# A blocked linear recurrence on one Trainium2 core: rewritten on 64x64 quarters of TensorE, with the tiles of 128 tokens in one pipeline

## The reference, cut to the recurrence

```
def _rwkv7_scan(r, w, k, v, a, b):           # [1, T, 8 heads, 64], state S is 64x64 per head
    def step(S, inp):
        r_t, w_t, k_t, v_t, a_t, b_t = inp
        sa = einsum('bhij,bhj->bhi', S, a_t)
        S = S * w_t[:, :, None, :] + sa[..., None] * b_t[:, :, None, :] + v_t[..., None] * k_t[:, :, None, :]
        y = einsum('bhij,bhj->bhi', S, r_t)
        return S, y
```

## Time and profile before

| | us |
|---|---|
| median of 3 runs (lowest, highest) | 3048.98 (3047.99, 3054.2) |
| the profiled execution, own time | 3055.45 |
| its span in the trace | 3053.7 |
| first instruction of the recurrence stage | 2567.17 |
| its last copy, L1819 | 2866.86 |

### The profile page before, as it was taken

How to read it: one execution, slowest core, us unless ns; L and a number is a source line. 1 busy time by engine, 2 the same in 40 slices (tenths; PEclk the granted TensorE clock), 3 DMA queues, 4 the chain that set the end, 5 groups by cost and what they waited for, 6 DMA issues and landing times. The chain is left out here.

```text
span 3053.7 us, 45425 instructions
## 1 busy us (share of the span) xinstructions
PE 2787.8 (91%) x18805; PEld 2297.6 (75%) x18805; DVE 1259.1 (41%) x2065; ACT 774.0 (25%) x1468; POOL 305.3 (10%) x256
## 2 busy tenths in 40 slices
PE   9799999999977898979999999996989987999866
PEld 8699999999965655758888888875767853888555
DVE  5333333333342567352333333336233334454546
ACT  6311111211151178242111111112111122222221
POOL 1100000000030034020000000005000001222102
PEclk9899999999998999979999999997999987999978
DMA  3211111111036400331111111113102100000032
GB/s 133 83 42 42 61 42 41 41 56 48 21 120 147 165 2 14 107 115 55 42 41 61 42 41 62 42 56 133 39 21 90 49 12 6 3 3 3 3 117 96
DMA packets 57934, 175.51 MB, mean 57 GB/s; under 512 B 7742, under 2 KB 15455, under 8 KB 56624
## 3 DMA queue, kind: packets, MB, share of 16 engines
q1 hardware_dynamic: 57778, 173.27, 17.3%
HBM read 146.30 MB, written 26.36 MB: 57 GB/s over the span
## 5 line engine op out<-in xcount | busy, mean ns | idle before, releaser
L769 PE MATMUL f0gu<-b1XH,f0w0H 128*128 128x346 f32 (+1 forms) x528 | 170.2, 322 | 13.5 <-DVE f0w0L L697 13.5
L712 DVE TENSOR_TENSOR f1hf<-f1sg,f1gu 128x512 f32<-128x512 f32 x44 | 30.3, 688 | 341.3 <-ACT f1sg L665 341.3
L723 DVE TENSOR_TENSOR Y<-f0dn,Y 128x512 f32<-128x512 f32 (+1 forms) x180 | 124.0, 689 | 113.6 <-PE f0dn L793 112.6
L771 PE MATMUL f0gu<-b1XH,f0w0L 128*128 128x346 f32 (+1 forms) x528 | 170.2, 322 | 0.0
L771 PE MATMUL f0gu<-b1XH,f0w1L 128*128 128x346 f32 (+1 forms) x528 | 169.7, 321 | 0.0
L770 PE MATMUL f0gu<-b1XL,f0w0H 128*128 128x346 f32 (+1 forms) x528 | 169.7, 321 | 0.0
L712 DVE TENSOR_TENSOR f0hf<-f0sg,f0gu 128x346 f32<-128x346 f32 (+1 forms) x66 | 34.1, 517 | 328.8 <-ACT f0sg L665 328.8
L769 PE MATMUL f0gu<-b1XH,f0w1H 128*128 128x346 f32 (+1 forms) x528 | 169.4, 321 | 0.0
L770 PE MATMUL f0gu<-b1XL,f0w1H 128*128 128x346 f32 (+1 forms) x528 | 169.0, 320 | 0.0
L769 PE MATMUL f1gu<-b1XH,f1w0H 128*128 128x512 f32 x352 | 139.2, 396 | 11.7 <-DVE f1w0L L697 11.7
L723 DVE TENSOR_TENSOR Y<-f1dn,Y 128x512 f32<-128x512 f32 x160 | 109.2, 690 | 90.7 <-PE f1dn L793 90.7
(11 more groups left out here) (391 smaller groups left out, 6521.2 us busy)
## 6 DMA issues: line engine op xcount, KB each, us to landing
f0raw<-in_w_gate_up SPq DMA_DIRECT2D x44, 512.0 KB, 5.3
f1raw<-in_w_gate_up SPq DMA_DIRECT2D x44, 512.0 KB, 5.2
residual<-Y SPq DMA_DIRECT2D x32, 512.0 KB, 2.8
Y<-in_w_ada SPq DMA_DIRECT2D x8, 1536.0 KB, 6.3
f0rawd<-in_w_down SPq DMA_DIRECT2D x22, 512.0 KB, 3.6
f1rawd<-in_w_down SPq DMA_DIRECT2D x22, 512.0 KB, 3.6
w_in_b_raw<-in_w_in_b SPq DMA_DIRECT2D x17, 512.0 KB, 3.6
w_in_a_raw<-in_w_in SPq DMA_DIRECT2D x12, 512.0 KB, 4.2
```

What stands on the lines that cost most here:

```text
L712: dve.tensor_tensor(hf[:, i, 0:w], sg[:, i, 0:w], gu[:, i, 1, 0:w], ALU.mult).then_inc(s["mul"], 1)
L723: dve.tensor_tensor(y, dn[0:r, (par * ND + i) % 4], y, ALU.add).then_inc(s["acc"], 1)
L769: pe.matmul(o, wH[c][:, j, k], xh, start=(k == 0), stop=False)
L771: last = pe.matmul(o, wL[c][:, j, k], xh, start=False, stop=(k == KC - 1))
```

## The change

The stage keeps its mathematics, and its operations are laid out anew:

- Member 1 of each pair is stored with its chunks exchanged (`at(e, q)` is `rows(q)` for e = 0 and `rows(1 - q)` for e = 1). So `p`, one of the two products of `xx`, `ab`, `ak`, `tx`, `wt` and the Gram matrices `rbk` go to all four quarters; the other product of `xx` and `mv`, `uu`, `sa`, `st`, `y` still use two at a time. A third Gram product per pair and chunk gives the triangular matrix already turned, so GpSimd's masking step moves to VectorE (`xm`).
- The transposes become ordinary float32 products with 64x64 identities, 64 per tile where there were 16 transposes of 128x128. `cum` is 8 products of 64 rows instead of 4 of 128. The state S is stored as 64-column blocks, and its products are 64x64. `rb`, `rk` and `y` are computed for each chunk alone.
- The ten groups (five levels by two pairs of heads `g`) become ten "halves". A pass over the ten halves holds the inverse of tile t, the chain and close of tile t-1, and the decays and start of tile t+1. On TensorE a half is: the other tiles' work, then `product(t, h)`, then `update(t, h - 1)`. On VectorE `added(h - 2)` stands first in half h, so an addition stands one half behind its update.
- VectorE and ScalarE operate on both members at once where they did each member by itself; GpSimd's `Uo` covers 128x512 elements instead of twice 128x256.
- The masks are loaded by two DMAs that write 64-column pieces at intervals of 128 columns.

```
+        def at(e, q):
+            return rows(q if e == 0 else 1 - q)
...
+                src = ins["cst"][:, C_TRIX64:C_END].rearrange("p (l t) -> p l t", t=H)
+                for i in range(2):
+                    sp.dma_start(cst[:, :, i], src).then_inc(s_in, 16)
...
+                def start(t):                                   # GpSimd
+                    da.wait(pool, t, "xm")
+                    pi.mark(pool.tensor_tensor(turned(t), turned(t), wide(eye), ALU.add), "eye")
+                    other(t, 1)
...
+                def added(t, h):                                # VectorE
+                    px.wait(dve, t, f"x{h}")
...
+                        if h < 2:
+                            if t:
+                                added(t - 1, HL + h - 2)
+                        elif t < NT:
+                            added(t, h - 2)
+                        if h == 0 and more: decayed(t + 1, "at")
+                        if h == 1 and more: decayed(t + 1, "bt")
+                        if h == 2 and more: decayed(t + 1, "kt")
+                        if h == 3: applied(t - 1, 0); masked(t + 1)
+                        if h == 4 and t: stepped(t - 1, 0); reads(t - 1)
+                        if h == 5: applied(t - 1, 1); decayed(t + 1, "rt")
+                        if h == 6 and more: keys(t + 1)
+                        if h == 7 and t: stepped(t - 1, 1)
...
+                def product(t, h):                              # TensorE
+                    po.wait(pe, t, f"u{l}")
+                    if h >= 2:
+                        dl.wait(pe, t, f"a{h - 2}")
+                    for cc in range(2):
+                        for q in range(2):
+                            for e in range(2):
+                                mm = pe.matmul(inv[at(e, q), g, e, ...], Uo[rows(q), slot(t, l), g, e, o], Xi(t, e, c, q), start=True, stop=True)
...
+                def update(t, h):
+                    al.wait(pe, t, f"m{h}")
+                    for cc in range(2):
+                        if l < LV - 1:
+                            for q in range(2):
+                                for e in range(2):
+                                    pe.matmul(inv[rows(q), g, e, ...], XT(t, e, c, q), mid[at(e, q), g, e, o], start=True, stop=True)
+                        for q, e in ((0, 0), (1, 0), (1, 1), (0, 1)):
+                            mm = pe.matmul(inv[at(e, q), g, 0, ...], mid[at(e, q), g, e, o], XT(t, e, c, q), start=True, stop=True)
...
+                steps = {1: ("ys0",), 3: ("sa0",), 4: ("st0", "rbk"), 5: ("sa1", "ys1"), 6: ("y0",), 7: ("st1",), 8: ("y1",)}
+                for t in range(NT + 1):
+                    for h in halves:
+                        if h == 0 and more: cum(t + 1)
+                        if h == 2 and t: closed(t - 1)          # wt, uu
+                        if t:
+                            for n in steps.get(h, ()): chain(t - 1, n)
+                        if h == 3: inner(t + 1)                 # ab and its turned copy
+                        if h == 6: keys(t + 1)                  # ak
+                        if h == 7: inverse_start(t + 1)         # tx
+                        if h == 8: turn(t + 1, (kk, ab), "tab")
+                        if h == 9: turn(t + 1, (k, v), "tkv")
+                        if h == 5 and t < NT: values(t)         # mv
+                        if t < NT: product(t, h)
+                        if h: update(t, h - 1)
+                        elif t: update(t - 1, HL - 1)
```

More of the change, by code:

```diff
@@ L1754, in recurrence_stage @@
[L1754 to L1760, removed]
@@ L1761, in recurrence_stage @@
-        dc = marks("dve_chain", ["sa0", "rb0", "rb1", "sx00", "sx01", "s00", "s01", "rk0", "rk1", "sa1", "sx10", "sx11", "s10", "s11"])
+        halves = range(HL)
+        pa = marks("pe_pre", ["cum", "ab", "ak", "tx", "tab", "tkv"])
+        pp = marks("pe_p", [f"p{h}" for h in halves])
+        px = marks("pe_x", [f"x{h}" for h in halves])
+        pm = marks("pe_mv", ["mv"])
+        pw = marks("pe_w", ["wt", "uu"])
+        pd = marks("pe_chain", ["ys0", "sa0", "st0", "rbk", "sa1", "ys1", "y0", "st1", "y1"])
@@ new lines, in recurrence_stage @@
+        aa = marks("act_pre", ["eex", "eneg", "ein", "xi", "tab", "tkv"])
+        al = marks("act_mid", [f"m{h}" for h in halves])
+        am = marks("act_mv", ["mv"])
+        aw = marks("act_w", ["wt", "uu"])
+        ad = marks("act_y", ["y"])
+        da = marks("dve_pre", ["at", "bt", "kt", "lt", "xm", "rt", "ak"])
+        dl = marks("dve_add", [f"a{h}" for h in halves])
+        dd = marks("dve_chain", ["sa00", "sa01", "sx0", "s0", "rb", "rk", "sa10", "sa11", "sx1", "s1"])
+        po = marks("pool_u", [f"u{l}" for l in range(1, LV)])
@@ L1796, in _ @@
                 pool.wait_ge(s_in, 32)
-                pool.tensor_scalar(tris[:, :], tri[:, :], -0.6065306597126334, None, ALU.mult).then_inc(s_c, 1)
-                for t in range(NT):
[L1800 to L1812, removed]
+                pool.tensor_scalar(tris[:, 0], cst[:, 2 + LV, 0], -0.6065306597126334, None, ALU.mult).then_inc(s_c, 1)
@@ L1814, in _ @@
+                def start(t):
+                    da.wait(pool, t, "xm")
+                    pi.mark(pool.tensor_tensor(turned(t), turned(t), wide(eye), ALU.add), "eye")
+                    other(t, 1)
+                start(0)
+                for t in range(NT):
+                    for l in range(2, LV):
+                        other(t, l)
+                    if t + 1 < NT:
+                        start(t + 1)
             @block.scalar
             def _(act):
[L1816 to L1819, removed]
@@ L1830, in _ @@
[L1830 to L1835, removed]
-                        else:
[L1837 to L1858, removed]
@@ new lines, in stepped @@
+                def stepped(t, q):
+                    pd.wait(dve, t, f"st{q}")
+                    pd.wait(dve, t, "ys1" if q else "ys0")
+                    dd.mark(dve.tensor_tensor(Sx[:, :, :], S[:, :, :], ch[:, 0:4 * H].rearrange("p (c t) -> p c t", c=4), ALU.add), f"sx{q}")
+                    dd.wait(dve, t, f"sx{q}")
+                    d = ein[:, t % 3, :, H * q + H - 1:H * q + H].broadcast_to([P, 4, H])
+                    dd.mark(dve.tensor_tensor(S[:, :, :], Sx[:, :, :], d, ALU.mult), f"s{q}")
@@ L1924, in _, with cum @@
             @block.tensor
             def _(pe):
-                def gram_of(bank, left, right, t, e, c):
-                    return pe.matmul(bank[:, P * c:P * (c + 1)], left[rows(e), c, tok(t)], right[rows(e), c, tok(t)], start=True, stop=True)
-                def gram64(bank, left, right, t, e):
+                def cum(t):
+                    if t:
+                        aa.wait(pe, t - 1, "tkv")
                     for c in range(4):
                         for q in range(2):
-                            mm = pe.matmul(bank[rows(q), H * c:H * (c + 1)], left[rows(e), c, chunk(t, q)], right[rows(e), c, chunk(t, q)], start=True, stop=True)
-                    return mm
@@ L1935, in chain, with gram @@
-                def chain(t, seg):
-                    if seg in (1, 3):
-                        q = seg // 2
-                        af.wait(pe, t, "wt")
+                            mm = pe.matmul(wk[:, q, P * c:P * (c + 1)], lw[rows(q), t, P * c:P * (c + 1)], tris[rows(q)].rearrange("p a t -> p (a t)"), start=True, stop=True)
+                    pa.mark(mm, "cum")
+                def gram(left, right, t, e, c, q, place, part):
+                    o = 4 * H * part + H * c
+                    return pe.matmul(wk[place, e, o:o + H], left[rows(e), c, chunk(t, q)], right[rows(e), c, chunk(t, q)], start=True, stop=True)
@@ new lines, in inner @@
+                def inner(t):
+                    da.wait(pe, t, "bt")
+                    if t >= 2:
+                        aw.wait(pe, t - 2, "wt")
+                    else:
+                        aa.wait(pe, t, "ein")
+                    for c in range(4):
+                        for q in range(2):
+                            for e in range(2):
+                                gram(ab, kk, t, e, c, q, at(e, q), 0)
+                            mm = gram(ab, kk, t, 1, c, q, rows(q), 1)
+                    pa.mark(mm, "ab")
@@ new lines, in turn @@
+                def turn(t, pair, n):
+                    aa.wait(pe, t, "xi" if n == "tab" else "tab")
+                    da.wait(pe, t, "kt")
+                    for c in range(4):
+                        for i, src in enumerate(pair):
+                            for q in range(2):
+                                for e in range(2):
+                                    mm = pe.matmul(wk[at(e, q), e, 4 * H * i + H * c:4 * H * i + H * (c + 1)], src[rows(e), c, chunk(t, q)], b.ident[rows(e), rows(e)], start=True, stop=True)
+                    pa.mark(mm, n)
@@ new lines, in values @@
+                def values(t):
+                    da.wait(pe, t, "ak")
```

(58 more changed lines are left out.)

486 lines of the change are left out of this document (269 added, 217 removed).

## The result

The changed kernel took 3035.01 us (median of 7 runs, 3030.16 to 3042.64), the kernel before 3050.71 on the same chip (7 runs, 3047.99 to 3055.07): 0.9942 of it, 95% interval 0.993 to 0.9954. That is 0.6% faster, where I forecast 2%; 3035 lies outside my range of 2968 to 3030.

A forecast was written before the change was run, and what follows sets the result against it. PE's in-order queue was taken as the bound. Start 20.7, pass 0 21, seven passes of 26.6 (186) and last chain 13.3 made 241 us against 300.3, 59 less: median forecast 2990 us, range 2968 to 3030.

The forecast's parts named there:

- 25.8 us per tile if nothing is late: TensorE's work per tile after the change: products by start distance and cum, 22.8 us, plus 3.0 us for waits.
- my 241: Whole stage after the change: 20.7 + 21 + 186 + 13.3 us, against 300.3 before.
- My 26.6 us: Time per tile in each of seven full passes, summed over ten halves with their waits; 35.9 us before.
- array sum of 22.8: TensorE per tile: four-quarter products at 30 ns, two-quarter at 58 ns, ab and cum, in us without waits.
- 0.8 us of stalls: At the pass's turn: 0.3 us in h0, cum waiting for the tkv copy, and 0.5 in h1, product waiting for VectorE's addition.
- 3.0 us for 60 waits: TensorE's semaphore waits per tile, charged at 0.05 us each.
- The addition's 1.0 us without cover: From an update's last start through VectorE's addition to the waiting product: 1.0 us, covered by other work in halves 2 to 9.
- Start and pass 0: Setup and serial start of tile 0, 20.7 us, then the first pass with no chain to cover additions, 21 us.
- Four quarters do not hold: Rival: in long runs products are issued no faster than one per 58 ns; 3055 us, slower than before; chance 0.09.
- quarters mixed, or waits in the halves: Rival: mixed groups in updates and p, or 0.3 us stalls per half, cost 3 us per tile; 3014 us; chance 0.2.
- The clock: Rival: TensorE's clock falls to 1.2 GHz in the passes, some 95 us slower than before; chance 0.04.
- three signs of being wrong: Four-quarter starts 58 ns per product apart, large PE idle ahead of products with VectorE as releaser, or clock 0.5 in a pass.

The follow-up runs named there:

- the two kernels that lengthened waits: The changed kernel with the product first in each half on TensorE, 3072.63 us; and with VectorE taking the addition of half h-1 first, 3059.1 us.

## Why the prediction was wrong

**The bound.** Right: only the stage changed, and TensorE's in-order queue set its time before. It is no longer TensorE's array that sets it after.

**The step that failed** is the sum "25.8 us per tile if nothing is late". It took PE's work as products by start distance and had no term for the arrival of the instructions: it put that at nothing. The reading that led there was `wt`: "the 16 of `wt` show no slackening". I had written beside it that `wt` is a burst "when the queue had time to fill". I saw the right objection and priced it as a slower rate of each product (58 ns, 3055 us). What the runs showed in its place is full rate inside a block and a next block of 256 instructions only every 3.8 us: 2,130 instructions are 8.4 packets, and 8.4 x 3.77 is the 31.7 us of a tile. The gaps are 9.1 of them, where I had charged 3.8 for waits and stalls; as the array's work is 0.2 less than I had, the net is 5.1 per tile in passes 1 to 5. Over all seven passes it is 31.5 us, most of the 41 by which the stage is longer than my 241. My 26.6 us would have asked for a block every 3.2 us. The trace before has one pair of packets 3.4 us apart and else none closer than 3.9, and no run here holds an average under 3.77 over five tiles. Counting instructions would have shown that I forecast a rate which the trace did not show anywhere.

**The terms by size.** My array sum of 22.8 was right: PE is busy 24.25 us per tile, and each of some 8.4 gaps leaves one 0.2 us tail of a matmul in that, 1.7 in all, so 22.6 are left, and with the 9.1 of gaps that is 31.7. The 0.8 us of stalls are there as forecast: waits for VectorE and ScalarE are 0.9 of the 9.1. The other 8.2 are the supply's, and the 3.0 us for 60 waits are not to be found beside them. That these hide in the gaps agrees with the two kernels that lengthened waits, and is worked out, not shown by itself. The addition's 1.0 us without cover was confirmed (49.9 us for 51), h1's 0.5 too (2.6 for 5), and `cum`'s stall was 0.45 instead of 0.3. GpSimd's operation of 512 columns is 1.3 us and not twice 0.73, at no cost or gain:

```profile
L1820 POOL TENSOR_TENSOR Uo<-LT,masks 128x512 f32<-128x512 f32 x6 | 7.8, 1295 | 29.5 <-PE inv_ps L2074 29.5
L1941 DVE TENSOR_TENSOR XX<-XX,inv_ps 128x512 f32<-128x512 f32 x8 | 5.5, 687 | 12.0 <-PE inv_ps L2088 12.0
```

**Start and pass 0** were 2.4 and 5.8 too low. The masks' DMA released its reader 4.26 us behind, where I had 3.7 (2.74 and 1). Tile 0's turns ran at a clock of 0.50, for which I had slowed only some terms. Pass 0 holds 2.7 us of "issue" idle, and its clock is 0.50 in its first 3 us and 0.75 to 0.80 from there until 2596. How these share the 5.8 I did not test. The other runs do not settle it: with `uu` five times the clock was low for 3.9 us of pass 0 instead of 8.0, and the pass still took 26.8; with two quarters at a time it was 1.00 throughout, and the pass took 23.6.

**The rivals.** "Four quarters do not hold" was wrong as worded (groups of 8 in 0.23 us). The one nearest in size, "quarters mixed, or waits in the halves" at 3014, named the wrong cause. The clock did not fall in passes 1 to 6 of the changed kernel. It was 0.50 for 3.4 us of its last chain (0.89 over 2826:2842), where I had expected 1.00, and it fell inside the passes of the two kernels with longer waits, and once, for 3.4 us, in the one with nine `wt`. Of the three signs of being wrong that I had named, none came in these passes: the idle time was there, but inside the groups and not ahead of the products.

The rule that I weighed, the Trainium skill's in "TensorEngine Tiling (Array Packing)", section "Gotcha 1: PSUM Pressure", on two row tiles in one PSUM bank, cost nothing that shows in four quarters either (0.23 to 0.25 us for 8 products, both row halves in both banks). The other, the 62 ns per MATMUL of the Trainium skill's "TensorE: Matmul & The Clock Gate", section "Wait — 56ns, not 53.3ns?", I had laid beside the wrong figure: it is per MATMUL, and the rival's 58 ns are per product of two. A product would take 124 ns by it, which the 58 ns in two quarters already exclude.

A page that I did not weigh bears on the cause: the Trainium skill, "Runtime: NRT & Kernel Launch", section "Instruction fetch mechanics", says that instructions arrive in blocks of 16 KiB, 256 of them, and that crossing a block is mostly hidden, since issue is slower than the filling. The trace agrees with the block (254 instructions per packet). On the hiding it agrees in a long run at two quarters (1.2 us idle in `uu` five times) and not in one at four (13.9), nor in the changed kernel's passes (32.3 us in five tiles).

**Open.** What holds a block back until at least 3.2 us after the one before it (3.8 on average) was not tried. With 10% fewer instructions the period fell by only 0.4 to 1.2; my estimate accounts for it, but no run tests it. Why the clock fell in the passes of three kernels was not tried either. The changed kernel also scatters more between runs (12 us) than that with transposes (3); I have no cause for it.

## What to carry to other kernels

Count instructions beside array time. A form that packs the array denser with small float32 products costs four instructions per product, and in these runs, where PE would use a block of 256 in less than about 3.8 us, the supply bounded it. Here 2,130 instructions per tile, not 22.8 us of array work, set 31.7. A short fast group does not tell the rate of a long one. In such a stretch added waits are cheaper than they look (3.6 us for ten of 1.0, at full clock), and saved instructions bring less than their share once the array or a copy stands behind them. Look at the granted clock of every tile before a longer period is put down to the edit.

## What the hardware showed that I had not expected

In the changed kernel a block of 256 PE instructions (16 KB on queue 8) was followed by a gap 42 times of 42: from 1.33 to 2.41 us after its packet's start, some 120 instructions in. Its packets stood 3.8 us apart on average, as they did with 52 and with 47 packets in five tiles, and in no run closer than 3.2. In a long run at four quarters (4 instructions in 29 ns) the gaps were 1.4 us; in one at two quarters (4 in 58 ns) they nearly vanish. Products alternating between pairs of quarters in short groups still ran at 0.27 to 0.29 us per 8. That a few products wait per quarter without holding up the others is my reading of it, which no run tests.
